# Norm steps: additions and low parts of every second feature tile on GpSimd

## What is computed

```python
def rmsnorm(t, g, eps=RMS_EPS):
    tf = t.astype(jnp.float32)
    tf = tf * lax.rsqrt(jnp.mean(tf * tf, axis=-1, keepdims=True) + eps)
    return (tf * g.astype(jnp.float32)).astype(t.dtype)

for i in range(DEPTH_2):
    hn = rmsnorm(h, g[0])
    m = rwkv_pool_mixer(hn, ...) if i % 2 == 0 else diff_attn_mixer(hn, ...)
    h = h + rmsnorm(m, g[1])
    f = sq_relu_mlp(rmsnorm(h, g[2]), mlp_w1[i], mlp_w2[i])
    h = h + rmsnorm(f, g[3])
return h[:, N_META:]
```

## Time and profile before

| | |
|---|---|
| median of 3 runs | 1908.32 us (1905.6 to 1911.94) |
| profiled execution: time | 1907.14 us |
| its span from first to last instruction | 1905.3 us |
| TensorE matmul busy | 1642.4 us (86%) |
| VectorE busy | 1091.5 us (57%) |
| ScalarE busy | 738.5 us (39%) |
| GpSimd busy | 114.4 us (6%) |
| mean granted TensorE clock | 0.90 |

### The profile page before, as it was taken

How to read it: one execution, slowest core, us unless ns; L and a number is a source line. 1 busy time by engine, 2 the same in 40 slices (tenths; PEclk the granted TensorE clock), 3 DMA queues, 4 the chain that set the end, 5 groups by cost and what they waited for, 6 DMA issues and landing times. The chain is left out here.

```text
span 1905.3 us, 35594 instructions
## 1 busy us (share of the span) xinstructions
PE 1642.4 (86%) x14964; PEld 1554.9 (82%) x14964; DVE 1091.5 (57%) x1639; ACT 738.5 (39%) x994; POOL 114.4 (6%) x139
## 2 busy tenths in 40 slices
PE   3999989858899988999886887779998989679997
PEld 2999979837888988999885775679997875579997
DVE  6994458868785465444465653554434446654434
ACT  2444346630005534553345000346433434346532
POOL 0121000002220000110000210000000020000000
PEclk7999999859999999999988995789999995589999
DMA  8895534303132353454341000234443430125451
GB/s 335 316 346 189 188 136 167 120 0 100 58 127 98 133 177 133 178 189 169 127 165 45 2 2 7 89 109 170 156 164 111 155 117 1 45 90 194 159 181 63
DMA packets 36992, 252.86 MB, mean 133 GB/s; under 512 B 4099, under 2 KB 5508, under 8 KB 7684
## 3 DMA queue, kind: packets, MB, share of 16 engines
q1 hardware_dynamic: 36436, 248.97, 36.6%
q10 hardware_dynamic: 432, 2.10, 0.3%
HBM read 250.00 MB, written 1.05 MB: 132 GB/s over the span
## 5 line engine op out<-in xcount | busy, mean ns | idle before, releaser
L430 DVE TENSOR_TENSOR w_lo<-raw,w_hi 128x2048 fp32r<-128x2048 f32 (+2 forms) x203 | 456.4, 2250 | 537.3 <-ACT w_hi L422 536.8
L496 PE MATMUL bank<-x_hi,w_hi 128*128 128x256 f32 (+1 forms) x2224 | 648.1, 291 | 64.5 <-DVE x_lo L645 38.7
L497 PE MATMUL bank<-x_lo,w_hi 128*128 128x256 f32 (+1 forms) x2224 | 640.3, 288 | 0.0
L498 PE MATMUL bank<-x_hi,w_lo 128*128 128x256 f32 (+1 forms) x2224 | 639.8, 288 | 0.0
L422 ACT ACTIVATE w_hi<-raw 128x2048 fp32r<-128x2048 f32 (+2 forms) x203 | 381.6, 1880 | 458.9 <-PE bank L498 423.1
L496 PEld LDWEIGHTS bank<-x_hi,w_hi 128*128 128x128 f32 x2224 | 429.2, 193 | 73.3 <-issue 65.2
L498 PEld LDWEIGHTS bank<-x_hi,w_lo 128*128 128x128 f32 x2224 | 430.9, 194 | 0.0
L497 PEld LDWEIGHTS bank<-x_lo,w_hi 128*128 128x128 f32 x2224 | 429.3, 193 | 0.9 <-issue 0.7
L496 PE MATMUL bank<-mh_hi,w_hi 128*128 128x272 f32 (+1 forms) x512 | 148.6, 290 | 6.5 <-PEq L2029 6.5
L498 PE MATMUL bank<-mh_hi,w_lo 128*128 128x272 f32 (+1 forms) x512 | 147.5, 288 | 0.0
L497 PE MATMUL bank<-mh_lo,w_hi 128*128 128x272 f32 (+1 forms) x512 | 147.2, 287 | 0.0
(11 more groups left out here) (425 smaller groups left out, 2162.5 us busy)
## 6 DMA issues: line engine op xcount, KB each, us to landing
raw<-in_stream SPq DMA_DIRECT2D x227, 1024.0 KB, 4.8
raw<-in_stream SPq DMA_DIRECT2D x8, 768.0 KB, 4.2
raw<-in_stream SPq DMA_DIRECT2D x4, 512.0 KB, 3.2
h<-in_h ACTq DMA_DIRECT2D x1, 1088.0 KB, 5.8
out<-h SPq DMA_DIRECT2D x8, 128.0 KB, 1.9
cst<-in_const ACTq DMA_DIRECT2D x1, 896.0 KB, 10.0
turning<-in_turning SPq DMA_DIRECT2D x1, 336.0 KB, 2.8
pool_w<-in_pool_w SPq DMA_DIRECT2D x1, 288.0 KB, 2.7
```

What stands on the lines that cost most here:

```text
L430: nc.vector.tensor_tensor(w_lo[:, s_at % 2, 0:kt], raw[:, r_at % RING, 0:kt], w_hi[:, s_at % 2, 0:kt].bitcast(F32), ALU.subtract).then_inc ...
L496: nc.tensor.matmul(out, hi, xh[:, k0 + k, 0:L], start=start, stop=False)
L497: nc.tensor.matmul(out, hi, xl[:, k0 + k, 0:L], start=False, stop=False)
L498: mm = nc.tensor.matmul(out, lo, xh[:, k0 + k, 0:L], start=False, stop=stop)
```

## The change

In the eight norm steps of the second half, the finish of tiles 1, 3, 5 and 7 goes to GpSimd (`on_pool`), as a plain addition or subtraction, counted by a semaphore of its own, `n_odd`. VectorE keeps all scalings and the finish of tiles 0, 2, 4 and 6. Whoever waits for tile k waits for both counts. The norms of the first half, with a column added (`b_cols`) or with another destination, stay as they were. `on_pool` is called in the GpSimd part of every block that has such a step.

```diff
@@ class Norm
-                lo_count[0] += DT if dst is None else 0
+                lo_count[0] += (DT // 2 if b_cols is None else DT) if dst is None else 0
+                self.shared, self.odd0 = dst is None and b_cols is None, odd_count[0]
+                odd_count[0] += DT // 2 if self.shared else 0
...
                     k = n - 2
-                    if k < 0 or self.dst is not None:
-                        continue
+                    if k >= 0 and self.dst is None and not (self.shared and k % 2):
+                        self.finish(dve, mid, k)
...
+            def on_pool(self, pool, mid):
+
+                L = self.L
+                if not self.shared:
+                    return
+                for k in range(1, DT, 2):
                     if self.add_to is not None:
-                        dve.wait_ge(n_mid, DT * self.q + k + 1)
-                        nc.vector.tensor_tensor(self.add_to[:, k], self.add_to[:, k], mid[:, k], ALU.add).then_inc(n_lo, 1)
+                        pool.wait_ge(n_mid, DT * self.q + k + 1)
+                        nc.gpsimd.tensor_tensor(self.add_to[:, k], self.add_to[:, k], mid[:, k], ALU.add).then_inc(n_odd, 1)
                     else:
...
+                        pool.wait_ge(n_hi, self.hi0 + k + 1)
+                        nc.gpsimd.tensor_tensor(x_lo[:, k, 0:L], mid[:, k], x_hi[:, k, 0:L].bitcast(F32), ALU.subtract).then_inc(n_odd, 1)
 
             def wait_tile(self, eng, k):
 
-                eng.wait_ge(n_lo, self.lo0 + k + 1)
+                eng.wait_ge(n_lo, self.lo0 + (k // 2 if self.shared else k) + 1)
+                if self.shared and k:
+                    eng.wait_ge(n_odd, self.odd0 + (k + 1) // 2)
@@ block of the mixer input
             @block.gpsimd
             def _(pool):
+                norm_in.on_pool(pool, mid_e)
                 pool.wait_ge(q["bon"], 1)
@@ def plain
+                @block.gpsimd
+                def _(pool):
+                    if before:
+                        before.on_pool(pool, mid)
+                    if norm:
+                        norm.on_pool(pool, mid)
```

More of the change, by code:

```diff
@@ L562, in dve_mod @@
             link(dve, "dve", nc.vector.tensor_tensor(mod[:, a:b], banks[7][:, a:b], col("b_ada", a, b - a), ALU.add))
-        norm_count, lo_count, hi_count = [0], [0], [0]
-        n_sq, n_sum, n_ms, n_y, n_mid, n_hi, n_lo = (sem(x) for x in ("n_sq", "n_sum", "n_ms", "n_y", "n_mid", "n_hi", "n_lo"))
+        norm_count, lo_count, hi_count, odd_count = [0], [0], [0], [0]
+        n_sq, n_sum, n_ms, n_y, n_mid, n_hi, n_lo, n_odd = (sem(x) for x in ("n_sq", "n_sum", "n_ms", "n_y", "n_mid", "n_hi", "n_lo", "n_odd"))
         def inverse_root(dve, act_wait, act_done, ms, y, tmp, out):
@@ L637, in on_dve, with finish @@
                     k = n - 2
-                    if k < 0 or self.dst is not None:
-                        continue
+                    if k >= 0 and self.dst is None and not (self.shared and k % 2):
+                        self.finish(dve, mid, k)
+            def finish(self, dve, mid, k):
+                L = self.L
+                if self.add_to is not None:
+                    dve.wait_ge(n_mid, DT * self.q + k + 1)
+                    nc.vector.tensor_tensor(self.add_to[:, k], self.add_to[:, k], mid[:, k], ALU.add).then_inc(n_lo, 1)
+                else:
+                    dve.wait_ge(n_hi, self.hi0 + k + 1)
+                    nc.vector.scalar_tensor_tensor(out=x_lo[:, k, 0:L], in0=mid[:, k], scalar=self.b_cols(k) if self.b_cols else 0.0,
+                                                   in1=x_hi[:, k, 0:L].bitcast(F32), op0=ALU.add, op1=ALU.subtract).then_inc(n_lo, 1)
@@ L640, in on_dve @@
+            def on_pool(self, pool, mid):
+                L = self.L
+                if not self.shared:
+                    return
+                for k in range(1, DT, 2):
                     if self.add_to is not None:
-                        dve.wait_ge(n_mid, DT * self.q + k + 1)
-                        nc.vector.tensor_tensor(self.add_to[:, k], self.add_to[:, k], mid[:, k], ALU.add).then_inc(n_lo, 1)
-                    else:
-                        dve.wait_ge(n_hi, self.hi0 + k + 1)
-                        nc.vector.scalar_tensor_tensor(out=x_lo[:, k, 0:L], in0=mid[:, k], scalar=self.b_cols(k) if self.b_cols else 0.0,
-                                                       in1=x_hi[:, k, 0:L].bitcast(F32), op0=ALU.add, op1=ALU.subtract).then_inc(n_lo, 1)
+                        pool.wait_ge(n_mid, DT * self.q + k + 1)
+                        nc.gpsimd.tensor_tensor(self.add_to[:, k], self.add_to[:, k], mid[:, k], ALU.add).then_inc(n_odd, 1)
+                    else:
+                        pool.wait_ge(n_hi, self.hi0 + k + 1)
+                        nc.gpsimd.tensor_tensor(x_lo[:, k, 0:L], mid[:, k], x_hi[:, k, 0:L].bitcast(F32), ALU.subtract).then_inc(n_odd, 1)
@@ L917, in _ @@
                 nc.scalar.activation(sp_t[:, 2], sp_t[:, 1], ACT.Exp, scale=-1.0).then_inc(ba_act, 1)
+            @block.gpsimd
+            def _(pool):
+                norm_mix.on_pool(pool, mid_m)
             @block.vector
```

## The result

The changed kernel took 1924.81 us (median of 4 launches, 1921.51 to 1929.27), the kernel before, run beside it on the same chip, 1906.96 us (4 launches, 1902.67 to 1911.94). The ratio is 1.0094, with a 95% interval of 1.0061 to 1.0127: slower by 18 us. Forecast were 1924.4 us and a chance of 0.77 for slower by over 0.3%.

A forecast was written before the change was run, and what follows sets the result against it. TensorE, busy 86% of the span, was taken to wait in norm steps for VectorE's tiles. Terms 10.0 + 0.3 + 0.7 + 5.1 = 16.1 us on 1908.3 gave 1924.4 us, range 1911 to 1935.

The forecast's parts named there:

- main term: Four low-part steps: GpSimd's subtraction for tile 7 queues behind VectorE's weight split, delaying TensorE by 10.0 us in all.
- tile 7 late, four steps: Low-part steps: first matmul of tile 7 later by 2.2, 2.6, 2.9 and 2.3 us, sum 10.0.
- three inner addition steps: Addition steps before the last: TensorE's totals of the next norm's squares end 0.1 us later each, 0.3 in all.
- last addition step: Addition step that ends the program, only stores behind it: its last addition comes 0.7 us later.
- clock: TensorE's pauses before tile 7 lower its granted clock: 1.7 us for three of four steps, 5.1 (bounds 0 and 6.8).
- The price of one GpSimd operation between two of VectorE's: Norm steps, shared SBUF ports: costs VectorE 0.64 + 0.29 - 0.415 = 0.51 us, more than the 0.355 saved.
- the extra semaphore waits and GpSimd's time: Shared norm steps: charged nothing, as GpSimd is idle there and the waiting queues wait longer for the tile itself.
- at the mixer input TensorE is at 1.2 GHz over the whole step anyway: Low-part step of the mixer input: reason for charging no clock loss there.
- the one price of 1.7: Work lost in 3.4 us at 1.2 GHz, read after one 2.38 us pause, charged for three low-part steps.
- rival 3: Norm steps: GpSimd gets nothing until VectorE's queue pauses; some 30 us slower, 1938 us; chance 0.06.
- Rival 1: Low-part steps: GpSimd's tile 7 slips in ahead of the weight split; 3.4 us slower, 1911.7 us; chance 0.17.
- Rival 2: Norm steps: VectorE and GpSimd don't contend; 4.6 us faster, 1903.7 us; chance 0.08.

The follow-up runs named there:

- e4: Changed kernel, but VectorE begins the weight split only once GpSimd's four low parts are done: 1913.97 us, ratio 1.0025.
- e5: Changed kernel, with the weight split that follows each low-part step issued in eight pieces: 1914.11 us, ratio 1.0032.
- e2: Changed kernel with only the four addition steps sharing tiles with GpSimd, all low parts on VectorE: 1906.84 us, ratio 0.9996.
- e6: Kernel before, with a semaphore increment on each of VectorE's three 128x1088 products: 1910.27 us, one execution.
- e9: Kernel before, with only the low parts of tiles 1, 3 and 5 at the mixer input on GpSimd: 1911.62 us, ratio 1.0013.
- e10: Kernel before, with each of VectorE's three 128x1088 products issued as four pieces of 128x272: 1912.41 us, one execution.
- e12: Kernel before, with GpSimd's own 128x1088 product issued as four pieces of 128x272: 1914.35 us, one execution.
- the seven executions above: Profiled executions whose low-part steps behind the mixer stand as in the kernel before; last three sections 615.1 us in the median, 616.8 in the one of before.
- e1: Changed kernel, with the low part of tile 7 back on VectorE in the four low-part steps: 1914.99 us, ratio 1.0028.

## Why the prediction was right

*The mechanism.* It rested on one comparison: VectorE's split starts at 6.3 us, GpSimd can ask at 6.5. The trace has 6.25 and 6.51. The main term follows from who is second: 2.63 us in place of 0.76. e4 and e5 brought back the 0.76 from two sides, by making the split wait and by making it short.

*The terms.*

| | forecast | measured |
|---|---|---|
| tile 7 late, four steps | 2.2 + 2.6 + 2.9 + 2.3 = 10.0 | 2.21 + 2.62 + 2.92 + 2.37 = 10.1 |
| three inner addition steps, first scaling to the next step's | +0.3 | +0.30, -0.55, -0.52, sum -0.8; ratio of e2 0.9996 |
| last addition step | +0.7 | +0.76 |
| clock | 1.7 x 3 = 5.1 | 1.53 + 1.56 + 2.50 = 5.6, and 0.9 at the mixer input |
| sum | 16.1 | 16.6 by these terms; 17.9 by the medians |

The terms are differences between single executions. Those of the inner addition steps lie within chance: the third of these stretches alone took 11.00 to 11.91 us in five executions that don't share there at all (before, e6, e9, e10, e12). And the 1.3 us between 16.6 and 17.9 need no forgotten term: by the median of the seven executions above, the last three sections are 15.2 us longer instead of 13.5.

The price of one GpSimd operation between two of VectorE's (0.51 us on top, from the earlier trace rows) is right: the scaling at 1264.60 is followed after 0.93, which is 0.64 + 0.29. What the forecast took as free, the extra semaphore waits and GpSimd's time, cost nothing that e2 can tell (4.4 us less to 2.9 us more).

*What was wrong, though it cost little.* First, "at the mixer input TensorE is at 1.2 GHz over the whole step anyway" let the clock cost nothing there. It does stand at 1.2 GHz over the step, but it then stays so longer: to 965.1, which is 14.7 us after the first scaling, where before it had risen some 8 us after it. Stretches of the step of the mixer input, after:

```profile
956.00:965.10 9.10, 7.33 (x33) 7.04 (x32) 2.91 (x3) 0.43 (x1) 2.68 (x2) 0.50 0.33 117
```

and before (first scaling at 956.48):

```profile
962.00:964.00 2.00, 2.00 (x10) 1.96 (x9) 2.00 (x3) 0.09 (x1) 0.00 (x0) 0.50 0.00 0
964.00:970.00 6.00, 6.00 (x47) 6.00 (x47) 1.22 (x2) 2.28 (x3) 0.00 (x0) 0.95 0.48 178
```

At this step the pause didn't make the clock fall; it was followed by a later rise. Second, the dips were not alike: 3.4 us at the first MLP as forecast, 6.65 us at the attention input:

```profile
1494.35:1501.00 6.65, 5.96 (x28) 5.99 (x29) 0.00 (x0) 0.00 (x0) 0.54 (x1) 0.50 0.47 158
```

The three come out between 1.5 and 2.5 us against the one execution of before; the one price of 1.7, from one pause, was near in the sum only. The 2.50 of the second MLP isn't one dip's: beside the 3.4 us behind its pause, the clock stands at 1.2 GHz some 100 us further on for 6.7 us, where before it was back at 2.4 GHz after 3.4 (0.50 from 1797.50 to 1800.80, 1.00 from 1800.90 to 1804.00),

```profile
1811.80:1818.50 6.70, 5.48 (x26) 5.51 (x27) 2.99 (x2) 1.93 (x2) 0.00 (x0) 0.50 0.51 166
```

and e5, which has no pause over 0.5 us, does the same there (0.50 from 1796.80 to 1803.60). Against the median of the seven executions the three are larger still, some 7 us in all (15.2 less 8.2 for tile 7; an estimate) where 5.1 were charged. So the pause, the dip behind it and the size of the first dip were right. The clock's sum, with the 0.9 us of the mixer input, was too small by 1 to 3 us. That the forecast came within 0.4 us of the median is in part luck: the change itself is only known to lie between 11.6 and 24.2 us. Third, rival 3 was dismissed with a distinction, drawn from the earlier trace rows, that doesn't hold: "GpSimd came between two operations that take a column scalar, as the scalings do". In the addition steps it came in ahead of an addition, which takes none. The conclusion stood, the reason didn't. Rival 3's own mechanism exists in the stretch of the earlier trace rows and three runs have not found what sets it off.

Rival 1 fell by 0.26 us, the lead of the split over the request; e4 is what it would have looked like: 0.25% over before (0 to 0.49%), where rival 1 had 3.4 us or 0.18%. Rival 2 (no contention) fell with the scalings of 1.00 us.

The Trainium skill, "SBUF — State Buffer", section "SBUF: two separate sides", has the pair of ports as a lock that goes to whoever starts first, for the whole instruction. In the low-part steps the traces agree: 2.63 us behind the whole split, 0.77 behind one piece of it. In the addition step that ends the program one request of GpSimd's was overtaken by an addition that VectorE began 0.23 us after it. Beside the three products they don't: with twelve pieces there, the rule gives GpSimd the ports after the first, and it ended 2.15 us after the twelfth. The rows decide, and the rule isn't safe to count on for a queue of such products.

## What to carry to other kernels

Work moved from VectorE to GpSimd has its price set by what stands next in VectorE's queue, not by GpSimd's speed: look for the longest operation on two SBUF tensors that can get ahead of it, and let either that operation wait (e4) or the last tile stay where it was (e1). Even so no division won anything here: each GpSimd operation put in between costs VectorE more (0.51 us) than it takes off it (0.355). And before you explain why a section is longer, profile the same program a second time: here 6.9 us of one section came and went with the clock. A single profile of the kernel before can mislead in the same way: this one was 1.7 us longer in its last three sections than the median of seven.

## What the runs showed of the hardware that was not expected

- Three products, or twelve pieces of them, kept GpSimd's product out to their end (5.68 and 6.30 us), while eight pieces of a weight split, also without waits between them, let its subtraction in after the first (0.77 us).
- In one of twelve meetings of two additions VectorE's went first, although it began 0.23 us after GpSimd's request (GpSimd's then took 1.23 us instead of 0.90).
- The recurrence stage of the mixer ran at a granted clock of 0.50 or 0.91 over the same 20 us in two executions of one program, and its section took 296.53 or 289.66 us. Launches of the kernel before spread from 1898.26 to 1917.35 us over all series, and from 1898.26 to 1915.3 within one.
- A pause of 2.3 us was followed by 3.4 us at 1.2 GHz in one step and by at least 6.65 us in another.
